# Scan output and second-pass x in long DRAM pieces, two stores moved to ScalarE's queue, landings waited for later

## The reference, cut to what matters

```python
y_a = ssd_branch(z, xbc, dt, ...)            # conv, chunked scan, silu gate, rms norm: 4096 wide
y_b = gelu(u) * (W_s @ layer_norm(gelu(v)))  # in chunks of 128 tokens: 2048 wide
merged = sigmoid(g_a) * (y_a @ w_branch_a) + sigmoid(g_b) * (y_b @ w_branch_b)
h = layer_norm(alpha * x + merged @ w_out)
# experts: per token 8 heads x 16 picked rows of peer_u and of peer_v (2048 wide each)
act = gelu(h . peer_u[e]);  out = layer_norm(alpha * h + sum(gate * act * peer_v[e]))
```

## Time and profile before

| | us |
|---|---|
| median of 3 runs | 5364.63 (5354.3 to 5366.88) |
| profiled execution | 5363.11, its span 5361.1 |
| PE busy (matmul) | 3604.4, 67% |
| DVE busy | 3353.5, 63% |
| POOL busy | 2561.5, 48% |
| ACT busy | 723.1, 13% |
| moved by DMA | 1672.06 MB, mean 312 GB/s |

### The profile page before, as it was taken

The page is one execution under the profiler, slowest core; times in us unless marked ns, Lnnn a source line. Parts: engine busy times, 40 slices in busy tenths (PEclk is TensorE's granted clock), DMA queues, the critical chain, the costliest instruction groups (busy, mean ns, idle before and its releaser), DMA issues. The chain is left out here.

```text
span 5361.1 us, 43672 instructions
## 1 busy us (share of the span) xinstructions
PE 3604.4 (67%) x16568; PEld 3025.1 (56%) x16568; DVE 3353.5 (63%) x3900; ACT 723.1 (13%) x1634; POOL 2561.5 (48%) x1569
## 2 busy tenths in 40 slices
PE   7999989999999898887787697897940000230000
PEld 5887778888887776776676686786730000000000
DVE  3554621000001679898866755565779999789999
ACT  2333321100000133333301110000110000000000
POOL 2676730000000345555533622443368888678885
PEclk8999999999999998999888898998975555565555
DMA  4666653344453399999998899999749999999998
GB/s 171 207 214 205 206 188 124 133 149 165 165 178 126 113 385 421 421 416 421 410 364 334 343 421 384 396 421 409 303 182 410 419 422 421 422 380 422 422 422 361
DMA packets 278120, 1672.06 MB, mean 312 GB/s; under 512 B 40000, under 2 KB 69248, under 8 KB 84992
## 3 DMA queue, kind: packets, MB, share of 16 engines
q0 software_dynamic: 160640, 1133.71, 51.7%
q1 hardware_dynamic: 117272, 535.57, 26.5%
HBM read 1633.31 MB, written 35.79 MB: 311 GB/s over the span
## 5 line engine op out<-in xcount | busy, mean ns | idle before, releaser
L524 PE MATMUL psum<-rows_a,w_ring 128*128 128x264 f32 x7168 | 1623.5, 388 | 25.2 <-PEq L482 18.9
L524 PEld LDWEIGHTS psum<-rows_a,w_ring 128*128 128x128 f32 x7168 | 1365.7, 191 | 265.7 <-issue 32.0
L524 PE MATMUL psum<-x_and_spare,w_ring 128*128 128x256 f32 x5632 | 1259.4, 385 | 112.2 <-PEq L482 80.8
L362 POOL DMA_INDIRECT rows_a<-in_peer_u,expert x388 | 808.4, 2083 | 921.0 <-DVE rows_a L417 856.7
L524 PEld LDWEIGHTS psum<-x_and_spare,w_ring 128*128 128x128 f32 x5632 | 1085.6, 194 | 271.5 <-issue 111.5
L417 DVE SCALAR_TENSOR_TENSOR rows_a<-rows_a,h_tokens 128x2048 f32<-128x2048 f32 x388 | 894.1, 2305 | 148.0 <-DMA rows_a<-in_peer_u,expert 93.2
L362 POOL DMA_INDIRECT rows_a<-in_peer_v,expert x384 | 588.9, 1534 | 282.9 <-DVE h_tokens L438 126.6
L438 DVE SCALAR_TENSOR_TENSOR h_tokens<-rows_a,coef,h_tokens 128x2048 f32<-128x2048 f32 x256 | 605.6, 2366 | 84.4 <-issue 76.4
L1904 PE MATMUL psum<-acc,selector 8*128 8x512 f32 x64 | 57.5, 1075 | 688.1 <-DVE rows_b L417 480.6
L202 POOL CAST rows_a<-rows_a 128x64 f32<-128x64 uint32 x8 | 1.9, 236 | 1012.8 <-DVE rows_a L195 1012.8
L1904 PEld LDWEIGHTS psum<-acc,selector 8*128 8x128 f32 x64 | 19.9, 325 | 724.4 <-DVE rows_b L417 486.9
(11 more groups left out here) (381 smaller groups left out, 3240.1 us busy)
## 6 DMA issues: line engine op xcount, KB each, us to landing
w_ring<-in_w_tiles SPq DMA_DIRECT2D x448, 1024.0 KB, 6.4
rows_a<-in_state_ssm POOLq DMA_DIRECT2D x32, 512.0 KB, 6.2
out_ssm_sample<-rows_a POOLq DMA_DIRECT2D x32, 512.0 KB, 4.4
rows_a<-acum_rows_dram SPq DMA_DIRECT2D x16, 512.0 KB, 6.2
smp_bc<-smp_bc_dram POOLq DMA_DIRECT2D x8, 1024.0 KB, 6.4
branch_b<-acum_rows_dram SPq DMA_DIRECT2D x16, 512.0 KB, 12.7
rows_a<-in_peer_u,expert POOLq DMA_INDIRECT x388, 20.5
rows_a<-in_xT SPq DMA_DIRECT2D x3, 2048.0 KB
```

Of the source, the lines that this page charges most:

```text
L362: return pool.indirect_dma_start(out=dst, out_offset=None, in_=table, in_offset=bass.IndirectOffsetOnAxis(ap=self.index(s), axis=0))
L524: last = pe.matmul(o, w[:, k * P:(k + 1) * P], x[:, k, :], start=start and k == 0, stop=stop and k == KB - 1)
```

## The change

1. The scan output gets one DRAM tensor per pass, laid out by partition: [128, 32, 264] in pass 0 and [128, 32, 256] in pass 1. `store_y` writes 4 blocks of a group side by side (in pass 1 one run of 4 KB per partition, before 4 runs of 1 KB); `load_ya` reads four blocks at once (4224 or 4096 bytes per partition, before 4 runs of 1056 or 1024).
2. x of pass 1, which pass 0 has already fetched into `x_and_spare`, is stored from there at the end of pass 0 to `x_rows` [128, 4096], and pass 1 fetches it from there for "out": 16 KB per partition in one run, before 16 runs of 1 KB.
3. The v rows (`v_last`) are sent by ACT right after the layer norm of v (ACT waits for its last row first), and are waited for in `back`, ahead of the gate ga. Before, SP sent them behind the weights of u tile 4.
4. `conv_prompt` is sent by ACT in the last group of pass 1, before SP sent it at the end of `ssd`. The last group's scan output and state are waited for in `sgu`, behind its first four weight loads, before at the end of `ssd`.

```diff
+        self.ys = [nc.dram_tensor(f"acts_by_token{i}", [P, G * GT, count * P + (NS if i == 0 else 0)], F32).ap()
+                   for i, (first, count) in enumerate(PASS_CHUNKS)]
+        self.x_rows = nc.dram_tensor("x_rows", [P, KB * P * PASS_CHUNKS[-1][1]], F32).ap()
...
+        self.x_next, self.v_out = nc.alloc_semaphore(name="x_next"), nc.alloc_semaphore(name="v_out")
+        self.last_out = nc.alloc_semaphore(name="last_out")
@@ ssd, SP @@
-                    sp.dma_start(ys_rows[:, GT * g:GT * (g + 1), ps.col:ps.col + np_],
-                                 yg[:, g % 2]).then_inc(y_out[g % 2], 16)
+                    sp.dma_start(self.ys[ps.i][:, GT * g:GT * (g + 1), 0:np_],
+                                 yg[:, g % 2]).then_inc(y_out[g % 2] if g < G - 1 else self.last_out, 16)
...
-                    sp.dma_start(dst, flat(S[:, g % 2])).then_inc(s_out[g % 2], 16)
+                    sp.dma_start(dst, flat(S[:, g % 2])).then_inc(s_out[g % 2] if g < G - 1 else self.last_out, 16)
...
+                for j in range(2):
+                    sp.wait_ge(y_out[j], 16 * (G // 2 - j))
+                    sp.wait_ge(s_out[j], 16 * (G // 2 - j))
                 if ps.last:
-                    sp.dma_start(out["conv_prompt"].rearrange("g p t k -> p g t k"), self.carry[:, ps.i]).then_inc(carry_out, 16)
                     sp.wait_ge(carry_out, 16)
-                for j in range(2):
-                    sp.wait_ge(y_out[j], 16 * (G // 2))
-                    sp.wait_ge(s_out[j], 16 * (G // 2))
@@ ssd, ACT @@
                     expert(g, 4)
+                    if ps.last and g == G - 1:
+                        self.wait_bank_read(act, grp(g, 5))
+                        act.dma_start(out["conv_prompt"].rearrange("g p t k -> p g t k"),
+                                      self.carry[:, ps.i]).then_inc(carry_out, 16)
@@ sgu, SP @@
+                sp.wait_ge(self.last_out, 32 * (ps.i + 1))
                 sp.dma_start(bs, a["sgu_b"]).then_inc(b_in, 16)
...
-                    if m == FT + 4:
-                        sp.wait_ge(ln["normed"], FT)
-                        if ps.smp:
-                            sp.dma_start(out["v_last"][:, :, P:P + NS], v[:, :, np_:n]).then_inc(v_out, 16)
-                        if ps.last:
-                            sp.dma_start(out["v_last"][:, :, 0:P], v[:, :, np_ - P:np_]).then_inc(v_out, 16)
-                if ps.smp or ps.last:
-                    sp.wait_ge(v_out, 16)
@@ sgu, ACT @@
                 gelu_u(1)
+                act.wait_ge(ln["normed"], FT)
+                if ps.smp:
+                    act.dma_start(out["v_last"][:, :, P:P + NS], v[:, :, np_:n]).then_inc(self.v_out, 16)
+                if ps.last:
+                    act.dma_start(out["v_last"][:, :, 0:P], v[:, :, np_ - P:np_]).then_inc(self.v_out, 16)
@@ back, SP @@
-                    src = self.ys[FT * half:FT * (half + 1), :, ps.col:ps.col + n].rearrange("k p t -> p k t")
+                    src = self.ys[ps.i][:, FT * half:FT * (half + 1), :]
...
-                self.load_x(sp, ps, xs, x_in)
+                if ps.last:
+                    sp.dma_start(xs.rearrange("p k t -> p (k t)"), self.x_rows).then_inc(x_in, 16)
+                else:
+                    self.load_x(sp, ps, xs, x_in)
@@ back, SP, behind the last weight load of pass 0 @@
+                if not ps.last:
+                    sp.wait_ge(self.x_next, 16)
+                    sp.dma_start(self.x_rows, self.shared[:, 0:KB * nxt.n]).then_inc(xr_out, 16)
+                    sp.wait_ge(xr_out, 16)
@@ back, ACT @@
+                    if c == FT:
+                        act.wait_ge(self.v_out, 16 * (ps.i + 1))
```

More of the change, by code:

```diff
@@ L592, in build @@
         self.pass_a, self.passes = passes[0], passes
-        self.x_next = nc.alloc_semaphore(name="x_next")
+        self.x_next, self.v_out = nc.alloc_semaphore(name="x_next"), nc.alloc_semaphore(name="v_out")
+        self.last_out = nc.alloc_semaphore(name="last_out")
         with self.root:
@@ L882, in ssd @@
         dord, pord = S_("dve", "pool")
-        ys_rows = self.ys.rearrange("n p t -> p n t")
         pos = lambda g, t: ps.pos + NT * g + t
@@ L1353, in sgu @@
         S_ = lambda *names: [self.sem("g_" + m) for m in names]
-        w_in, b_in, w0_in, v_out, masked, turned, tok_ready, mixed, mix_read, gated = S_(
-            "w_in", "b_in", "w0_in", "v_out", "masked", "turned", "tok_ready", "mixed", "mix_read", "gated")
+        w_in, b_in, w0_in, masked, turned, tok_ready, mixed, mix_read, gated = S_(
+            "w_in", "b_in", "w0_in", "masked", "turned", "tok_ready", "mixed", "mix_read", "gated")
         dord, pord = S_("dve", "pool")
@@ L1374, in _ @@
                         sp.wait_ge(smp_done, 1)
-                        sp.dma_start(self.ys.rearrange("n p t -> p n t")[:, 0:G * GT, ps.col + np_:ps.col + n],
+                        sp.dma_start(self.ys[ps.i][:, :, np_:n],
                                      smp.y[:].rearrange("p g t b -> p (g t) b")).then_inc(smp_out, 16)
-                    if m == FT + 4:
-                        sp.wait_ge(ln["normed"], FT)
-                        if ps.smp:
-                            sp.dma_start(out["v_last"][:, :, P:P + NS], v[:, :, np_:n]).then_inc(v_out, 16)
-                        if ps.last:
-                            sp.dma_start(out["v_last"][:, :, 0:P], v[:, :, np_ - P:np_]).then_inc(v_out, 16)
-                if ps.smp or ps.last:
-                    sp.wait_ge(v_out, 16)
                 if smp:
@@ L1547, in back @@
         S_ = lambda *names: [self.sem("b_" + m) for m in names]
-        keys_in, x_in, hs_out, sc_out, merge_done, turned, turn_read = S_(
-            "keys_in", "x_in", "hs_out", "sc_out", "merge_done", "turned", "turn_read")
+        keys_in, x_in, xr_out, hs_out, sc_out, merge_done, turned, turn_read = S_(
+            "keys_in", "x_in", "xr_out", "hs_out", "sc_out", "merge_done", "turned", "turn_read")
         ya_in = [self.sem(f"b_ya_in{j}") for j in range(8)]
```

## The result

The changed kernel took 5321.0 us (median of 4 runs, 5319.3 to 5325.3), the kernel before 5365.8 on the same chip (4 runs, 5354.3 to 5370.4): ratio 0.9921, 95% interval 0.9904 to 0.9938. That is 45 us faster, where 59 were forecast against 5365; the range of 5277 to 5342 held it. The profiled execution has a span of 5318.9 us, 42.2 less than before.

What follows compares the result with a forecast made beforehand. Pass 1 was taken as bound by DMA bytes at 421 GB/s, so only idle time or bytes count. 5363.1 - 38 - 2 - 15 + 1 - 3 - 1 = 5305, forecast as 5306 us, range 5277 to 5342.

Steps and rivals of the forecast that it cites:

- rival 3: sgu of pass 1: the v_last store still holds up weights from ACT's queue, the 15 us stay; 5321 us, chance 0.06.
- The rival that all stalls go in full: Whole kernel: bytes are not the limit and every stall is saved, 98 us; 5267 us, chance 0.08.
- Back of pass 1, -38: "wb", "wa", "out" of pass 1: long pieces of y_a and x save 38 us, bounds 17 and 43.
- 64 steps ... 208.7 MB: "wb" to "out": bytes needed, with 64 steps of two gathers, total 208.7 MB, 495.7 us at 421 GB/s.
- 8.4 more than needed: "wb" to "out": the 217.1 MB moved exceed the need by 8.4, taken as gathers filling eight buffers during stalls.
- the lower bound's 23: "wb" to "out": only idle DMA time goes, 23 us, less some 6 for new small waits, 17.
- rival 1: back of pass 1: only idle time goes, filling buffers is no gain, 17 instead of 38; 5327 us, chance 0.17.
- `v_last`, -15: sgu of pass 1: sending v_last from ACT, some 17 us earlier, saves 15 us, bounds 7 and 18.7.
- `ssd`, -2: ssd of pass 1: stores in 1024 packets of 4 KB instead of 4096 of 1 KB save 2 us, bounds 0 and 2.5.
- Barriers, -3 and -1: Barriers behind ssd: moved waits save 3 us in pass 0 (0 to 4), 1 us in pass 1 (0 to 9).
- Store of x_rows, 0: End of pass 0: the 2 MB store is covered by SP's 16.3 us barrier wait and costs 0.
- rival 4: x_rows store and load: flat DMAs stay on one engine, store needs 80 us; slower, 5406 us, chance 0.04.

Runs made afterwards that it cites:

- extra8: Changed kernel plus four copies of x_rows (2 MB each) to a DRAM scratch tensor, issued by ACT in pass 1; ratio to the kernel before 0.9959.
- x_short: Changed kernel with x read from its input in runs of 1 KB in both passes and no x_rows; ratio to the kernel before 0.9932.
- v_last_early: Changed kernel with v_last issued on SP behind u tile 2, when the last scaling round ends; ratio to the kernel before 0.9916.
- v_last_sp: Changed kernel with v_last issued on SP again, behind u tile 4; ratio to the kernel before 0.9945.
- y_only: Kernel before with only the long pieces of the scan output, and v_last's landing waited for in back; ratio to the kernel before 0.9967.
- y_short: Changed kernel with pass 1's scan output rows padded by 64 bytes, so stores and loads run over 1 KB; ratio to the kernel before 0.9963.
- after_again: Changed kernel, unedited, run and profiled a second time; median 5318.1 us, ratio to the kernel before 0.9916.
- waits_back: Changed kernel with conv_prompt on SP again and all waits back at the barrier behind ssd; ratio to the kernel before 0.9915.
- q_early3: Changed kernel with three expert steps of the "out" tiles moved to q tiles 3, 5 and 7; ratio to the kernel before 0.9929.

## Why the prediction was right, and where its sizes were off

The mechanism was right and one of its sizes was not: 45 us came where 59 were forecast. The measured 5321 happens to be the number of rival 3, but `v_last` gave its 15 us, so that is chance; the difference lies in `back`.

**Bytes as the limit of `back`: right.** 421 GB/s flat in the three stretches, and 8.4 MB added by extra8 cost 22 us. The rival that all stalls go in full (5267) is out.

**Back of pass 1, -38: mis-sized, -26.6.** The step that failed is "64 steps ... 208.7 MB" with "8.4 more than needed. During each stall the gathers ran ahead". The steps were counted by the table of tiles, and I took the surplus for filling. The issues over 3264:3803 of before and over 3247:3760 of the changed kernel (line, engine, count, us to landing):

```profile
rows_a<-in_peer_u,expert POOLq DMA_INDIRECT x67, 17.7
rows_a<-in_peer_v,expert POOLq DMA_INDIRECT x66, 18.2
```

```profile
rows_a<-in_peer_u,expert POOLq DMA_INDIRECT x67, 27.6
rows_a<-in_peer_v,expert POOLq DMA_INDIRECT x66, 27.8
```

133 gathers passed in both, not 128: when PE begins "wb", DVE still has two steps of the gates to do (in before, two dot products of the gates stand between 3264 and DVE's first "wb" tile at 3279), and by the last "out" tile it has caught up, 66 steps in all. Five gathers are 5.2 of the 8.4 MB. All in all 217.07 MB passed in the one and 215.95 in the other. Only the idle time could go, 539 - 217.07 / 0.421 = 23.4 us, and 1.1 MB of filling, 2.7: 26.1. That is the lower bound's 23 without the "some 6 for new small waits", which cost nothing: PE's 14.15 us at 3631 are longer than the wait for y_a that went, while DMA ran at 421. For x alone filling does count: x_short moved 1.36 MB more before the first q tile. So rival 1 (5327) had the right quantity, the idle time, and took too much off it; 26.6 lies about halfway between its 17 and the forecast's 38. The three stretches took 513 us, where "some 500" was given as a sign. Of the 26 us, y_a's long pieces bring 17 to 19 and x_rows 8 to 9; the two add up.

**`v_last`, -15: right in size (330.9 to 316.0, means 330.1 to 314.9), half in its reason.** That the store is issued some 17 us earlier, when gathers have stopped, carries it; "the weights no longer stand behind it" does not, since v_last_early keeps it on SP and loses nothing measurable. Rival 3, that the 15 us stay, fails by the `sgu` column: 313.9 to 317.5 us wherever ACT sends the store. The Trainium skill (DMA: Bandwidth & Descriptors, section Issuing engines are not separate DMA queues) says that another issuing engine saves only the issue time; v_last_early agrees, with 317.7 against 313.9 to 317.5 on ACT. Of the 15 us, 7 to 8 are shown to be the moment of the issue. The other 7 are open: before has 330, but v_last_sp and y_only, which send v_last from the same place with y in long pieces, 322 and 324. Their bytes and packets in `sgu` are the same as before's, and no run separates what they do differently. In y_only the 17.3 us of `back` and some 6.5 of `sgu` make 24, inside its interval of 9 to 27 but above its 18.

**`ssd`, -2: not there.** It took 826.3 and 824.2 before, 825.6 and 825.5 after, 821.9 in y_short with the short pieces. That is within what executions differ by.

**Barriers, -3 and -1, and ACT's wait, +1.** PE's idle time at the first barrier fell from 9.04 to 6.44 and the one at 2705 from 18.89 to 17.6, in size as predicted. At 2705 the reason was another. The prediction gave the 1 us to gathers that land sooner, and expected the barrier 4 to 6 us behind the last one. The last gather did not land sooner (10.5 us after its issue, before 9.1); what went was the wait for `conv_prompt`, and the barrier came 1.5 to 1.7 us behind the gather. The stage that ends there does not show the gain. ACT's wait showed as one of 0.24 us on PE in pass 0.

But pass 0 as a whole gained nothing: the profiled execution was 3.8 us ahead at the barrier and level at 1879. Part of it went at the layer norm before q. The stretch 1709:1712 of before and of the changed kernel:

```profile
1709.00:1712.00 3.00, 2.24 (x10) 1.95 (x11) 3.00 (x3) 2.88 (x3) 0.00 (x0) 1.00 0.34 145
```

```profile
1709.00:1712.00 3.00, 3.00 (x9) 2.32 (x9) 1.45 (x2) 2.82 (x4) 0.00 (x0) 0.55 0.02 8
```

In this stretch the granted clock is 1.00 in before and 0.55 in the changed kernel, near its lower level of 1.2 GHz. Both had the same wait of 2.53 us just ahead of it, and the 32 matmuls of the variance took 9.07 us for 7.39. In after_again they took 7.39 and pass 0 took 1133.6, like before, so this varies by execution. Whether the edit takes part is open: the four executions with the old waits at the first barrier (before twice, y_only, waits_back) have 1132.8 to 1134.3 us in the table's first column, the ten with the new waits 1133.4 to 1138.5, six of them over 1136. The means, 1133.6 and 1135.7, differ by nearly as much as the barrier gained.

**Store of x_rows, 0: right.** It landed under SP's wait for the barrier, 10.4 us of it. With it rival 4 is out, which needed over 74 us.

The sum by stages, from the means of before and after, is `back` -26.6, `sgu` -15.1, `ssd` 0 and first barrier -2.6, of which pass 0 takes back some or all: -42 to -44 for the 45 measured. No kernel tried beats the changed one by more than the intervals tell.

## What to carry to other kernels

Where DMA is the limit, count the bytes that pass a stretch in the trace, not those that a plan says it needs: the gain of removing stalls is the idle time of the DMA engines, and the stalls themselves can remain. Short runs hurt by what they keep from the transfers behind them in their own queue. So lengthen the runs of a load towards those it shares turns with (here 4 and 16 KB beside 8 KB), or issue it when the others rest; from which engine it is sent mattered less here than when. A wait of several things is worth what the second to last leaves.

## What the runs showed of the hardware

The same 1 MB in 2048 runs of 512 bytes landed in 6.0 to 9.5 us from ACT (after, q_early3, y_short) and 9.8 from SP (v_last_early) while gathers rested. Issued from SP 11 us later in the stage, beside gathers, it took 28.6 (v_last_sp).

The first four loads of y_a, 512 KB each, landed in 18.7 to 23.8, 27.2 and 35.8 to 35.9 us (medians) for runs of 4, 2 and 1 KB beside gathers of 8 KB. That is far less than in proportion to the number of packets, as turns of one packet each with the 8 KB gathers would have it (1183 and 1190 packets in y_short's 24 us). The second four do not keep this order: 18.9 to 19.2 us for 4 KB, 26.0 for 2 KB, 22.5 and 21.6 for 1 KB, and no run says why.

The median landing of the gathers over "wb" to "out" was 27.6 us in the changed kernel and 17.7 in before, at nearly the same bytes. No run tells whether that is the longer packets beside them or the full use of the engines.

A barrier opened 1.5 us behind the landing of the last gather, with no plain DMA left to wait for.
